# The second block's output projection by seven block products for three of four tile pairs

## The chip, the cores and the metric

The program runs on one core of a Trainium2 chip. The metric is the device time of one execution in microseconds. Five engines work side by side and meet at semaphores: TensorE (matmul), VectorE, ScalarE, GpSimd, and SyncE, which issues most DMAs. In profile rows they are PE (PEld for its weight loads), DVE, ACT, POOL and SP.

## The reference

Two transformer-like blocks follow each other on x of 1024 tokens by 1024 features, in float32. The change is in the second block, at the line that multiplies by w_out:

```
br_a = neighbourhood_attention(q, k, v, rpb) @ w_na_out
br_b = silu(layernorm(conv(c_a * sigmoid(c_b)))) @ w_conv_out
merged = sigmoid(g_a) * br_a + sigmoid(g_b) * br_b
x = x + merged @ w_out
h2 = rmsnorm(x, norm2_g)
up = dwconv3(h2 @ w_up)
gate, val = split(up)
x = x + (gelu(gate) * val) @ w_down
```

merged and w_out are 1024x1024.

## The kernel before

x is kept transposed, as eight tiles x_t[:, d, :] of 128 features by 1024 tokens. Each float32 product is made of three matmuls of a rounded type: high by high, high by low, low by high. So every operand is split first: a rounding makes the high part, a subtraction the low part.

The stages around the change are these.

- The branch stage (TensorE, line 2008). For each of the eight output tiles d TensorE makes both branches, 48 matmuls of 512 columns, into four banks of PSUM. VectorE multiplies each by its gate and adds the two (`merge`, lines 3776 to 3781), ScalarE rounds the merged tile (line 2777) and VectorE makes its low part (`mix2_low`, line 3785).
- The output projection (TensorE, `product`, line 1449). For each of eight tiles of w_out, 8 slices of the contraction x 3 matmuls x 2 halves of the tokens = 48 matmuls. GpSimd splits each weight tile (lines 1261 and 1269), one ahead of TensorE. VectorE adds the result to x (`enter`, line 3345). ScalarE stores x to DRAM, squares it (line 2422), and VectorE sums the squares (`add_alone`, line 3337) for the norm.
- The FFN's first product already uses the seven-product scheme (Winograd's form of Strassen's): a pair of weight tiles and the two halves of the tokens make a 2x2 block product out of seven block products instead of eight. Its operands are direct parts of x (b11, b21, b22) and mixed ones (t1 to t4). VectorE makes their sums and low parts (`h_combos`, lines 3303 to 3325) and ScalarE the high ones (line 2396). The contraction's slices go in pairs of tiles kk and kk+4, in the order 0, 1, 3, 2 (`PAIR_ORDER`), and the tiles of the output projection in the same order (`ORDER`: 0, 4, 1, 5, 3, 7, 2, 6). In `enter` VectorE makes the parts of the first pair after its fourth addition of a tile and those of the second after its fifth; `tile 6` and `tile 7` of the text are the last two in this order.
- Behind them, the loop over FFN pairs: TensorE line 1738, weight sums and low parts on GpSimd (lines 1294 to 1318), high parts on ScalarE (line 2414), convolution taps on VectorE (lines 3836, 3840), GELU on ScalarE (line 2796).

Each engine works through its own list in the order in which the code is written; there is no scheduler.

## Time and profile before

| | us |
|---|---|
| median of 3 runs | 2425.54 |
| lowest, highest | 2425.41, 2428.5 |
| the profiled execution | 2427.07 |
| its span | 2425.3 |
| PE busy | 2401.6 (99%) |
| DVE busy | 1896.2 (78%) |
| ACT busy | 960.4 (40%) |
| POOL busy | 1358.6 (56%) |

The span is what the records cover; the profiled execution's own time is 1.8 us longer. A busy share is an average over stages with different limits, so it doesn't tell what bounds one of them. In every slice of the page but the first TensorE is at 9 tenths.

### The profile page before, as it was taken

To read this page: it belongs to the slowest core of one execution; us is meant where nothing else is said; L and a number is where in the kernel's file an instruction comes from. 1 tells how busy PE (TensorE), PEld (TensorE's weight loads), DVE (VectorE), ACT (ScalarE), POOL (GpSimd) and SP (SyncE) were. 2 spreads that over 40 slices of the span, in tenths; PEclk is the share of its full clock that TensorE was granted. 3 is DMA by queue.
4 is the path that set the end of the run, shared out by engine and by line. 5 is a ranking of instruction groups with operands and counts; after the bars stand their busy time and mean duration, and the time that the engine had idled before them with its cause. 6 is when DMAs were issued, how large, how long until landed. Compare 5 with 4: busy or idle time off the path is not lost.

```text
span 2425.3 us, 37420 instructions
## 1 busy us (share of the span) xinstructions
PE 2401.6 (99%) x13845; PEld 1979.7 (82%) x13845; DVE 1896.2 (78%) x1915; ACT 960.4 (40%) x1319; POOL 1358.6 (56%) x791
## 2 busy tenths in 40 slices
PE   8999999999999999999999999999999999999999
PEld 8788887888888788887877788888888888887887
DVE  6766666776667888888877889354799999999998
ACT  5344445353333533324333331311355455443444
POOL 3322222369887777772322223333379999978786
PEclk9999999999999999999999999999999999999999
DMA  6111112234444755431311111113222222235332
GB/s 228 36 35 43 35 35 97 104 125 157 151 155 172 256 170 155 151 126 36 131 41 35 39 35 52 44 52 124 93 87 78 86 88 85 78 130 183 104 113 92
DMA packets 243636, 244.79 MB, mean 101 GB/s; under 512 B 16943, under 2 KB 212186, under 8 KB 238810
## 3 DMA queue, kind: packets, MB, share of 16 engines
q1 hardware_dynamic: 214916, 166.70, 21.9%
q10 hardware_dynamic: 28630, 76.86, 8.3%
q8 instruction: 59, 0.97, 0.2%
q14 instruction: 31, 0.25, 0.0%
HBM read 181.13 MB, written 64.17 MB: 101 GB/s over the span
## 4 chain that ended last, share of the span: by engine, by line
PE 86%; DVE 8%; ACT 2%; issue 2%; POOL 1%; DMA 0%; DVEq 0%; SPq 0%; ACTq 0%; POOLq 0%
PE psum L1449 30%; PE psum L1738 26%; PE psum L1858 11%; PE psum L2106 7%; PE psum L2008 3%; PE psum L1487 2%; PE psum L1574 1%; PE psum L1512 1%; PE psum L1920 1%; PE psum L1939 1%; DVE x_t L3373 1%; DVE sq_sum_gain L3580 0%; POOL ffn_s_lo L1318 0%; PE psum L1634 0%; DVE sq_sum L3337 0%
## 5 line engine op out<-in xcount | busy, mean ns | idle before, releaser
L1261 POOL CAST w_hi<-w_raw 128x1024 fp32r<-128x1024 f32 x85 | 98.6, 1160 | 769.0 <-issue 386.2
L1449 PE MATMUL psum<-h_hi,w_hi 128*128 128x512 f32 x1040 | 329.9, 398 | 1.3 <-DVE h_lo L3040 1.1
L1449 PE MATMUL psum<-h_lo,w_hi 128*128 128x512 f32 x1040 | 321.5, 390 | 0.0
L1449 PE MATMUL psum<-h_hi,w_lo 128*128 128x512 f32 x1040 | 321.1, 390 | 0.0
L1449 PEld LDWEIGHTS psum<-h_hi,w_lo 128*128 128x128 f32 x1040 | 195.3, 188 | 41.9
L1449 PEld LDWEIGHTS psum<-h_lo,w_hi 128*128 128x128 f32 x1040 | 195.2, 188 | 41.7
L1269 POOL TENSOR_TENSOR w_lo<-w_raw,w_hi 128x1024 fp32r<-128x1024 f32 x85 | 220.0, 2588 | 9.5 <-DVE h_lo L3040 2.8
L1449 PEld LDWEIGHTS psum<-h_hi,w_hi 128*128 128x128 f32 x1040 | 189.2, 188 | 39.5 <-issue 1.8
L3634 DVE SCALAR_TENSOR_TENSOR conv_t<-u_t,cols,conv_t 128x1024 f32<-128x1024 f32 x120 | 175.1, 1459 | 2.6
L1318 POOL TENSOR_TENSOR ffn_s_lo<-ffn_s_sum,ffn_s_hi 128x512 fp32r<-128x512 f32 x84 | 159.8, 1933 | 7.0 <-ACT ffn_s_hi L2414 4.0
L1738 PE MATMUL psum<-ffn_t_hi,ffn_s_hi 128*128 128x512 f32 x252 | 98.0, 389 | 0.0
L1738 PE MATMUL psum<-ffn_t_lo,ffn_s_hi 128*128 128x512 f32 x252 | 98.0, 389 | 0.0
L1738 PE MATMUL psum<-ffn_t_hi,ffn_s_lo 128*128 128x512 f32 x252 | 98.0, 389 | 0.0
L1318 POOL TENSOR_TENSOR mlp_s_lo<-mlp_s_sum,mlp_s_hi 128x512 fp32r<-128x512 f32 x60 | 95.0, 1612 | 2.6 <-ACT mlp_s_hi L2414 2.6
L1858 PE MATMUL psum<-down_part_hi,down_hi_odd 128*128 128x512 f32 x228 | 88.7, 389 | 0.0
L1858 PE MATMUL psum<-down_part_lo,down_hi_odd 128*128 128x512 f32 x228 | 88.7, 389 | 0.0
L1858 PE MATMUL psum<-down_part_hi,down_lo_odd 128*128 128x512 f32 x228 | 88.7, 389 | 0.0
L3490 DVE TENSOR_TENSOR down_part_lo<-down_part_raw,down_part_hi 128x1536 fp32r<-128x1536 f32 (+2 forms) x31 | 70.4, 2270 | 8.5 <-ACT down_part_hi L2550 8.5
L1858 PE MATMUL psum<-down_part_hi,down_hi_even 128*128 128x512 f32 x196 | 76.3, 389 | 0.1
L1858 PE MATMUL psum<-down_part_hi,down_lo_even 128*128 128x512 f32 x196 | 76.3, 389 | 0.0
L1858 PE MATMUL psum<-down_part_lo,down_hi_even 128*128 128x512 f32 x196 | 76.3, 389 | 0.0
L2414 ACT ACTIVATE ffn_s_hi<-ffn_s_sum 128x512 fp32r<-128x512 f32 x84 | 48.3, 624 | 63.8 <-POOL ffn_s_sum L1296 55.8
(625 smaller groups left out, 6865.6 us busy)
## 6 DMA issues: line engine op xcount, KB each, us to landing
w_raw<-in_w_in SPq DMA_DIRECT2D x120, 256.0 KB, 3.0
w_raw<-in_w_up SPq DMA_DIRECT2D x76, 256.0 KB, 3.3
act_parts<-act_mixed ACTq DMA_DIRECT2D x15, 1024.0 KB, 3.8
down_part_raw<-act_parts SPq DMA_DIRECT2D x14, 1024.0 KB, 5.6
down_part_raw<-act_parts SPq DMA_DIRECT2D x15, 768.0 KB, 6.4
ffn_raw<-in_w_up SPq DMA_DIRECT2D x44, 256.0 KB, 3.3
ffn_rows<-ffn_gate ACTq DMA_DIRECT2D x22, 512.0 KB, 2.6
ffn_part_raw<-ffn_rows SPq DMA_DIRECT2D x18, 512.0 KB, 4.3
```

What stands on the lines that cost most here:

```text
L1261: pool.tensor_copy(hi, raw).then_inc(weight_hi, 1)
L1269: pool.tensor_tensor(lo, raw, hi.bitcast(F32), ALU.subtract).then_inc(weight_split, 1)
L1318: done = pool.tensor_tensor(lo[:, :], full[c], hi[:, :].bitcast(F32), ALU.subtract)
L1449: last = pe.matmul(psum[:, first_bank + t, :], w, a[:, k, t * HALF:(t + 1) * HALF], start=(k == order[0] and j == 0), stop=(k == order[-1] ...
L1487: last = pe.transpose(psum[:, dst_bank + c // 4, (c % 4) * P:(c % 4 + 1) * P], block_in, ident[:, :])
L1738: last = pe.matmul(psum[:, bank, :], w, a[:, :], start=start and kk == part[0] and j == 0, stop=stop and kk == part[-1] and j == 2, skip_g ...
L1858: done = pe.matmul(psum[:, bank, :], w, b, start=first and i == 0 and k == 0, stop=last and i == len(window) - 1 and k == 2)
L2008: last = pe.matmul(psum[:, bank + t, :], w, a[:, t * HALF:(t + 1) * HALF], start=(k == 0 and j == 0), stop=(k == 3 and j == 2))
L2106: done = pe.matmul(psum[:, bank, 0:tokens.stop - tokens.start], w, b, start=first and i == 0 and k == 0, stop=last and i == len(window) - ...
L2414: act.activation(stage.weights[s][c][0][:, :], src, ACT.Copy).then_inc(weight_combo_hi, 1)
L3490: dve.tensor_tensor(part_lo[f % 3][:, here, :], part_raw[f % 3][:, here, :], part_hi[f % 3][:, here, :].bitcast(F32), ALU.subtract).then_i ...
L3634: dve.scalar_tensor_tensor(acc, u_t[:, c % 2, tap:tap + SEQ], w, acc, ALU.mult, ALU.add)\
```

## The change

The weight tiles of the output projection are taken in pairs. Three of the four pairs are made by seven block products with the two halves of the tokens, 12 matmuls each (4 pairs of slices x 3), and the fourth (tiles 6 and 7) stays as it was.

- In the branch stage the tiles are merged in the order 0, 4, 1, 5, ... (`MIX_ORDER`), and after each second one VectorE makes four sums, and ScalarE and VectorE the high and low parts of t1 to t4.
- GpSimd makes the factors of a pair (`out_pair_factors`): four sums and seven low parts of 128x512; ScalarE makes the seven high parts (`out_factor_hi`).
- TensorE begins the first pair with what doesn't need the last merged tiles (`ahead2`).
- VectorE adds each block product to every part of x that holds it (`out_pair`): ten additions for a pair.
- The squares of the tiles 1, 2 and 3 go through a buffer of half a tile (`square_halves`).
- The FFN parts of the first two pairs of tiles are made after the third pair of the projection is added, not between the additions.

```diff
+MIX_ORDER = tuple(d for kk in range(KT // 2) for d in (kk, kk + KT // 2))
+MIX_SUMS = ("t1", "t3", "t2", "t4")
+MIX_LOWS = ("t4", "t2", "t1", "t3")
+OUT_PAIRS = 3
+MIX_0, OUT_0, WSUM_0, HIGH_0, FACTOR_0 = 2, 1, 5, 1, 16
+OUT_SEVEN = ("b11", "b21", "t4", "t2", "t1", "b22", "t3")
+OUT_FACTOR = {"b11": "a11", "b21": "a12", "t4": "a22", "t2": "s2", "t1": "s1", "b22": "s4", "t3": "s3"}
+OUT_BANK = {"b11": 0, "t1": 1, "t3": 2, "t2": 3, "t4": 4, "b21": 5, "b22": 6}
+OUT_WSUMS = (("s1", "s2", "s3", "s4"), ("s1", "s2", "s4", "s3"))
+OUT_HIGHS = (("a11", "a12", "s1", "s2", "a22", "s3", "s4"), ("a11", "a12", "a22", "s1", "s2", "s4", "s3"))
+OUT_LOWS = (("a11", "a12", "s1", "s2", "s3", "a22", "s4"), ("a11", "a12", "a22", "s1", "s2", "s4", "s3"))
...
-                ([], KT // 2, lambda i: [branches(i * 2 * P + j * P) for j in range(2)], []),
+                ([], KT // 2, lambda i: [branches(i * P + j * HALF) for j in range(2)], []),
...
+                elif isinstance(n, int) and T_OUT2 + 2 <= n < T_FFN:
+                    sp.wait_ge(weight_split, n - n % 2)
...
+                if i == 0:
+                    add("s1")
+                    low("a11")
+                    low("a12")
+                    pool.wait_ge(tile_done, T_OUT2)
+                    add("s2")
+                    low("s1")
+                    low("s2")
+                    add("s3")
+                    low("s3")
+                    low("a22")
+                    add("s4")
+                    raw_read("a22")
+                    low("s4")
+                    return
+                for name in ("a11", "a12", "a22"):
+                    low(name)
+                out_piece_done(pool, i - 1, "t1")
+                add("s1")
+                add("s2")
+                low("s1")
+                out_piece_done(pool, i - 1, "b22")
+                add("s4")
+                low("s2")
+                out_piece_done(pool, i - 1, "t3")
+                add("s3")
+                raw_read("s2")
+                low("s4")
+                low("s3")
...
-            def out_tile2(d, part=range(KT), split=None):
-                return product(T_OUT2 + d, d % 2, 2 * (d % 2), mix2_hi, mix2_lo, part, split=split)
+            def out_seventh(i, name, part=range(KT // 2)):
+                factor = OUT_FACTOR[name]
+                pe.wait_ge(out_factor, FACTOR_0 + out_nth(OUT_LOWS, i, factor))
+                for kk in part:
+                    if name[0] == "b":
+                        pe.wait_ge(mix_split, KT + 2 * kk + (2 if name[1] == "2" else 1))
+                        p, d, half = mix2_direct(kk, name)
+                        hi, lo = mix2_hi[p, d, half], mix2_lo[p, d, half]
+                    else:
+                        pe.wait_ge(mix_part_lo, MIX_0 + 4 * kk + MIX_LOWS.index(name) + 1)
+                        hi, lo = mix2_parts[kk][name][0][:, :], mix2_parts[kk][name][1][:, :]
+                    at_k = slice(kk * P, (kk + 1) * P)
+                    wh, wl = out_w[factor][0][:, at_k], out_w[factor][1][:, at_k]
+                    for j, (w, a) in enumerate(((wh, hi), (wh, lo), (wl, hi))):
+                        last = pe.matmul(psum[:, OUT_BANK[name], :], w, a, start=kk == 0 and j == 0,
+                                         stop=kk == KT // 2 - 1 and j == 2)
...
+            def out_bank_read(i, name):
+                if name in ("b22", "t3"):
+                    pe.wait_ge(x_added, KT + 2 + 2 * i + (1 if name == "b22" else 2))
+                else:
+                    pe.wait_ge(out_read, OUT_0 + 8 * i + {"b11": 2, "b21": 3, "t4": 4, "t2": 6, "t1": 8}[name])
+            ahead2, last2 = range(KT // 2 - 1), [KT // 2 - 1]
             pe.wait_ge(branch_a, KT - 1)
-            pe.wait_ge(branch_b, KT - 1)
-            out_tile2(0, split=lambda k: (mix_split, KT + k + 1))
-            for d in range(1, KT - 1):
-                if d >= 2:
-                    pe.wait_ge(x_added, KT + 2 + d - 1)
-                out_tile2(d)
-            pe.wait_ge(x_added, KT + 2 + KT - 2)
+            out_seventh(0, "b11", ahead2)
+            pe.wait_ge(branch_a, KT)
+            out_seventh(0, "b21", ahead2)
+            out_seventh(0, "t1", ahead2)
+            pe.wait_ge(branch_b, KT)
+            out_seventh(0, "t2", ahead2)
+            out_seventh(0, "t3", ahead2)
+            out_seventh(0, "b11", last2)
+            out_seventh(0, "b21", last2)
+            out_seventh(0, "t4")
+            out_seventh(0, "t2", last2)
+            out_seventh(0, "t1", last2)
+            out_seventh(0, "b22")
+            out_seventh(0, "t3", last2)
+            for i in range(1, OUT_PAIRS):
+                for name in OUT_SEVEN:
+                    out_bank_read(i - 1, name)
+                    out_seventh(i, name)
+            def out_tile2(d, part=range(KT)):
+                return product(T_OUT2 + d, d % 2, 2 * (d % 2), mix2_hi, mix2_lo, part)
+            out_bank_read(OUT_PAIRS - 1, "t1")
+            out_tile2(KT - 2)
+            out_bank_read(OUT_PAIRS - 1, "t3")
...
+            def square_halves(e):
+                act.wait_ge(x_added, ffn.added + e + 1)
+                spill_x(ORDER[e])
+                if e >= 2:
+                    act.wait_ge(sq_summed, ffn.sums + e - 1)
+                act.activation(sq_half[:, :], x_t[:, ORDER[e], 0:HALF], ACT.Square).then_inc(sq_half_ready, 1)
+                act.wait_ge(sq_half_added, OUT_0 + e)
+                act.activation(sq_half[:, :], x_t[:, ORDER[e], HALF:], ACT.Square).then_inc(sq_ready, 1)
+            square_alone(ffn, 0)
+            square_halves(1)
+            out_arrived(2)
+            out_factor_hi(2, *OUT_HIGHS[1])
+            for e in (2, 3):
+                square_halves(e)
+            out_piece_done(act, OUT_PAIRS - 1, "t3")
+            square_alone(ffn, 4)
+            for kk in PAIR_ORDER[:2]:
+                for names in (DIRECT, MIXED):
+                    h_combos_hi(ffn, kk, names)
+            square_alone(ffn, 5)
+            enter(ffn, 4, 5, eps2, range(KT - 2, KT - 1))
...
+            def mix2_sums(kk):
+                dve.wait_ge(merged, 2 * kk + 2)
+                b11, b12, b21, b22 = (sig_a[:, d, half] for d in (kk, kk + KT // 2) for half in (left_half, right_half))
+                t1, t2, t3, t4 = (mix2_parts[kk][name][2][:, :] for name in ("t1", "t2", "t3", "t4"))
+                dve.tensor_tensor(t1, b12, b11, ALU.subtract).then_inc(mix_summed, 1)
+                dve.tensor_tensor(t3, b22, b12, ALU.subtract).then_inc(mix_summed, 1)
+                dve.wait_ge(mix_summed, MIX_0 + 4 * kk + 2)
+                dve.tensor_tensor(t2, b11, t3, ALU.add).then_inc(mix_summed, 1)
+                dve.wait_ge(mix_summed, MIX_0 + 4 * kk + 3)
+                dve.tensor_tensor(t4, b21, t2, ALU.subtract).then_inc(mix_summed, 1)
...
+            for n in range(KT):
+                merge(n)
+                if n % 2:
+                    mix2_sums(n // 2)
+                    mix2_low(n - 1)
+                    mix2_low(n)
+                    mix2_parts_low(n // 2)
...
+                out_piece_done(dve, i, "b11")
+                add(both[0], twice("b11"))
+                add(both[1], twice("b11"))
+                out_piece_done(dve, i, "b21")
+                add(x_t[:, a, left_half], bank("b21"), after=1)
+                out_piece_done(dve, i, "t4")
+                add(x_t[:, b, left_half], bank("t4"), after=2)
+                for e in ((), (1,), (2, 3))[i]:
+                    square_halves_added(e)
+                out_piece_done(dve, i, "t2")
+                add(x_t[:, a, right_half], bank("t2"), after=1)
+                add(both[1], twice("t2"), after=4)
+                out_piece_done(dve, i, "t1")
+                add(x_t[:, a, right_half], bank("t1"), after=5)
+                add(x_t[:, b, right_half], bank("t1"), after=6)
+                out_piece_done(dve, i, "b22")
+                add(x_t[:, a, right_half], bank("b22"), x_added, after=7)
+                out_piece_done(dve, i, "t3")
+                add(both[1], twice("t3"), x_added, after=8)
 
             dve.wait_ge(x_back, 16 * 2)
-            enter(ffn, lambda e: 2 * (e % 2))
-            left_half, right_half = slice(0, HALF), slice(HALF, SEQ)
+            for i in range(OUT_PAIRS):
+                out_pair(i)
+            for kk, alone in zip(PAIR_ORDER[:2], (4, None)):
+                for names in (DIRECT, MIXED):
+                    h_combos(ffn, kk, names)
+                if alone is not None:
+                    dve.wait_ge(x_added, ffn.added + alone + 1)
+                    add_alone(ffn, alone)
+            enter(ffn, lambda e: 2 * (e % 2), range(KT - 2, KT))
```

VectorE's list at the end of the projection shows the last point. Names: ffn_t_0 and ffn_b_0 are mixed and direct parts of the FFN's first pair, sq a squared tile. Before:

```order
L3345 TENSOR_TENSOR x_t<-x_t,psum 128x1024
L3337 TENSOR_TENSOR sq_sum<-sq_sum,sq 128x1024
L3303 TENSOR_TENSOR ffn_t_0_sum<-x_t 128x512
L3325 SCALAR_TENSOR_TENSOR ffn_b_0_lo<-x_t,cols,ffn_b_0_hi 128x512
L3325 SCALAR_TENSOR_TENSOR ffn_t_0_lo<-ffn_t_0_sum,cols,ffn_t_0_hi 128x512
L3325 SCALAR_TENSOR_TENSOR ffn_b_0_lo<-x_t,cols,ffn_b_0_hi 128x512 x2
L3307 SCALAR_TENSOR_TENSOR ffn_t_0_sum<-x_t,cols,ffn_t_0_scaled 128x512
L3310 SCALAR_TENSOR_TENSOR ffn_t_0_sum<-x_t,cols,ffn_t_0_sum 128x512
L3312 SCALAR_TENSOR_TENSOR ffn_t_0_sum<-x_t,cols,ffn_t_0_sum 128x512
L3323 TENSOR_TENSOR ffn_t_0_lo<-ffn_t_0_sum,ffn_t_0_hi 128x512 x3
L3345 TENSOR_TENSOR x_t<-x_t,psum 128x1024
L3337 TENSOR_TENSOR sq_sum<-sq_sum,sq 128x1024
```

The third pair of VectorE's additions, and what stands behind them now:

```order
L4070 TENSOR_TENSOR x_t<-x_t,psum 128x1024 x3
L4070 TENSOR_TENSOR x_t<-x_t,psum 128x512 x2
L4052 TENSOR_TENSOR sq_sum<-sq_sum,sq_half 128x512
L4054 TENSOR_TENSOR sq_sum<-sq_sum,sq_half 128x512
L4052 TENSOR_TENSOR sq_sum<-sq_sum,sq_half 128x512
L4054 TENSOR_TENSOR sq_sum<-sq_sum,sq_half 128x512
L4070 TENSOR_TENSOR x_t<-x_t,psum 128x512
L4070 TENSOR_TENSOR x_t<-x_t,psum 128x1024
L4070 TENSOR_TENSOR x_t<-x_t,psum 128x512 x3
L4070 TENSOR_TENSOR x_t<-x_t,psum 128x1024
L3531 TENSOR_TENSOR ffn_t_0_sum<-x_t 128x512
L3553 SCALAR_TENSOR_TENSOR ffn_b_0_lo<-x_t,cols,ffn_b_0_hi 128x512
```

(The first of the three additions of 1024 columns belongs to the second pair.) The FFN parts have moved behind six tiles' additions, and two additions a pair have become ten.

On GpSimd, the end of the branch stage's loop and the first weight tile of the projection, before (w_hi and w_lo are the split tile):

```order
L1262 REGISTER_ALU
L1269 TENSOR_TENSOR w_lo<-w_raw,w_hi 128x1024
L870 REGISTER_ALU
L870 COMPARE_AND_BRANCH
L1261 CAST w_hi<-w_raw 128x1024
L1269 TENSOR_TENSOR w_lo<-w_raw,w_hi 128x1024
```

and the factors of the first pair, behind the branch stage's last tile, now (out_w_a are direct factors, out_w_s and out_first_s sums):

```order
L1295 TENSOR_TENSOR out_first_s_700<-w_raw 128x512
L1300 TENSOR_TENSOR out_w_a_lo<-w_raw,out_w_a_hi 128x512 x2
L1295 TENSOR_TENSOR out_first_s_701<-out_first_s_700,w_raw 128x512
L1300 TENSOR_TENSOR out_w_s_lo<-out_first_s_700,out_w_s_hi 128x512
L1300 TENSOR_TENSOR out_w_s_lo<-out_first_s_701,out_w_s_hi 128x512
L1295 TENSOR_TENSOR out_w_s_sum<-w_raw 128x512
L1300 TENSOR_TENSOR out_w_s_lo<-out_w_s_sum,out_w_s_hi 128x512
L1300 TENSOR_TENSOR out_w_a_lo<-w_raw,out_w_a_hi 128x512
L1295 TENSOR_TENSOR out_w_s_sum<-w_raw,out_first_s_701 128x512
L1300 TENSOR_TENSOR out_w_s_lo<-out_w_s_sum,out_w_s_hi 128x512
```

A CAST and a subtraction of a whole tile each have become eleven operations of half a tile for two tiles.

## Rows read from the trace of the kernel before

**Rows 1.** Busy time by stretch: us, then each engine's busy us (x instructions), clock, DMA
```profile
core 0: us, PE busy (x) PEld busy (x) DVE busy (x) ACT busy (x) POOL busy (x), PEclk, DMA share, GB/s
1585.30:1673.00 87.70, 87.13 (x385) 71.81 (x384) 48.40 (x33) 13.54 (x13) 28.65 (x16) 1.00 0.16 48
1673.00:1760.40 87.40, 87.40 (x387) 72.39 (x386) 54.78 (x45) 22.62 (x32) 32.30 (x18) 1.00 0.37 133
```

**Rows 2.** Timeline, PE: start us, us, operation, in brackets the idle time before
```profile
1673.21 0.62 PE L1449 MATMUL psum<-mix_hi,w_hi 128*128 128x512 f32 x2
...
1760.25 0.39 PE L1738 MATMUL psum<-ffn_b_hi,ffn_first_a_hi 128*128 128x512 f32 x1
...
1839.91 0.50 PE L1738 MATMUL psum<-ffn_b_hi,ffn_s_hi 128*128 128x512 f32 x1 [1.56 <-DVE ffn_z_val L3894]
```

**Rows 3.** Waits of PE from 1600 to 2190: us in total, times, longest
```profile
PE psum L1738 <- DVE ffn_z_val L3894: 1.6, 1, 1.6
```

**Rows 4.** Timeline, DVE, around the last addition of a tile
```profile
1758.41 2.30 DVE L3337 TENSOR_TENSOR sq_sum<-sq_sum,sq 128x1024 f32<-128x1024 f32 x1
1760.64 1.21 DVE L3345 TENSOR_TENSOR x_t<-x_t,psum 128x1024 f32<-128x1024 f32 x1
```

**Rows 5.** Chain of waits after it: start us, us, what
```profile
1781.56 1.46 POOL ffn_a_lo L1318
...
1819.64 1.05 ACT ffn_gate L2796
```

**Rows 6.** Timeline, POOL and DVE at the same times
```profile
1767.96 1.29 POOL L1294 TENSOR_TENSOR ffn_s_sum<-ffn_raw 128x512 f32<-128x512 f32 x1 [8.33 <-DMA ffn_raw<-in_w_up]
1769.33 1.60 POOL L1296 TENSOR_TENSOR ffn_s_sum<-ffn_s_sum,ffn_raw 128x512 f32<-128x512 f32 x1
...
1769.84 1.64 DVE L3310 SCALAR_TENSOR_TENSOR ffn_t_sum<-x_t,cols,ffn_t_sum 128x512 f32<-128x512 f32 x1
...
1795.62 2.16 POOL L1296 TENSOR_TENSOR ffn_s_sum<-ffn_s_sum,w_raw 128x512 f32<-128x512 f32 x1
...
1796.54 0.67 DVE L3888 TENSOR_TENSOR third_sum<-second_sum,psum 128x512 f32<-128x512 f32 x1
```

**Rows 7.** Timeline, POOL's split of the last branch tile, and DVE
```profile
1663.78 2.40 POOL L1269 TENSOR_TENSOR w_lo<-w_raw,w_hi 128x1024 fp32r<-128x1024 f32 x1
...
1678.07 2.43 DVE L3785 TENSOR_TENSOR mix_lo<-sig_a,mix_hi 128x1024 fp32r<-128x1024 f32 x2
...
1707.38 3.40 DVE L3337 TENSOR_TENSOR sq_sum<-sq_sum,sq 128x1024 f32<-128x1024 f32 x1
```

**Rows 8.** DMA issues, 1640 to 1800: count, KB each, median us to landing
```profile
w_raw<-in_w_out SPq DMA_DIRECT2D x16, 256.0 KB, 3.0
x_t<-x_spill ACTq DMA_DIRECT2D x1, 4096.0 KB, 13.3
```

**Rows 9.** Timeline, DVE, FFN parts of the first three pairs
```profile
1721.58 0.68 DVE L3303 TENSOR_TENSOR ffn_t_sum<-x_t 128x512 f32<-128x512 f32 x1
1723.40 0.75 DVE L3325 SCALAR_TENSOR_TENSOR ffn_b_lo<-x_t,cols,ffn_b_hi 128x512 fp32r<-128x512 f32 x1 [1.14 <-ACT ffn_b_hi L2396]
...
1728.41 4.82 DVE L3323 TENSOR_TENSOR ffn_t_lo<-ffn_t_sum,ffn_t_hi 128x512 fp32r<-128x512 f32 x3
...
1745.29 1.90 DVE L3323 TENSOR_TENSOR ffn_t_lo<-ffn_t_sum,ffn_t_hi 128x512 fp32r<-128x512 f32 x3
...
1751.97 1.78 DVE L3303 TENSOR_TENSOR ffn_t_sum<-x_t 128x512 f32<-128x512 f32 x1
```

**Rows 10.** Busy time and granted clock (PEclk) around two waits of PE
```profile
384.00:386.00 2.00, 1.00 (x14) 0.88 (x15) 2.00 (x4) 1.81 (x4) 0.90 (x1) 1.00 0.00 0
386.00:388.00 2.00, 2.00 (x8) 1.55 (x7) 1.82 (x3) 1.50 (x3) 1.92 (x2) 0.54 0.03 8
388.00:390.00 2.00, 2.00 (x71) 1.64 (x70) 2.00 (x3) 0.86 (x1) 0.60 (x1) 0.60 0.03 6
...
1840.00:1842.00 2.00, 2.00 (x9) 1.63 (x10) 2.00 (x2) 0.87 (x2) 2.00 (x3) 1.00 0.00 0
```

157 lines of the change are left out of this document (137 added, 20 removed).

## The prediction

> **What bounds the kernel now.** I read the busy shares by stretch first. In the stretch of the output projection TensorE is busy for 87.40 of 87.40 us and VectorE for 54.78 [rows 1], which looks like a stage bound by TensorE. Its first matmul starts at 1673.21 and the first of the next stage at 1760.25 [rows 2]: 87.04 us for 384 matmuls, 0.2267 us each.
>
> The timeline of VectorE says more. It has idle time early in the stage, but none at its end: the addition of squares before the last addition of a tile ends at 1760.71, and that last addition (x_t<-x_t,psum, the eighth) starts at 1760.64 [rows 4] (a record overlaps the next one slightly). TensorE's last tile ended at the same moment. The two engines tie there.
>
> The chain of waits from there on leaves TensorE: last addition, sums for the mixed parts on VectorE, table loads and rounding on ScalarE, low parts on GpSimd, ScalarE's GELU behind them, and VectorE again, until TensorE itself waits 1.56 us at 1839.91 [rows 2, 5]. Between 1600 and 2190 TensorE has no other wait [rows 3]. So the kernel's end moves by as much as this chain moves, and the chain starts with the last addition. I call the start of that addition L; before, L = 1760.64. A TensorE that is done earlier gains nothing unless L is earlier.
>
> **What TensorE saves.** Three pairs by seven block products are 3 x 7 x 4 x 3 = 252 matmuls of 512 columns, and two plain tiles 96: 348 for 384. 36 x 0.2267 = 8.2 us are gone. That is the most that the change can give.
>
> **What a contended operation costs.** The new work is on VectorE and GpSimd, and the rows show that these two hold each other up. A GpSimd half-tile operation (128x512) takes 1.29 us alone, a VectorE one with two SBUF inputs 0.75 [rows 6, 9]; where both have a queue, they alternate, and each takes 1.60 to 1.64 us [rows 6]: with the step between them some 1.7 us for one of each. A VectorE operation of 1024 columns takes 1.2 us alone (2.43 for two), and 3.40 when it meets a whole-tile operation of GpSimd [rows 7]. An addition from PSUM is not held: 0.67 us while GpSimd was in an operation of 2.16 [rows 6].
>
> The Trainium skill (GPSIMD Engine Reference, Key points) says the same of the interfaces: GpSimd contends with VectorE instructions that have two SBUF inputs, and so not with an addition whose second input is PSUM. The trace agrees, with 0.67 us. Were the PSUM additions held too, the sum would be that of the third rival below.
>
> **The branch stage.** Each pair of tiles gets four sums and four low parts of 512 columns more on VectorE, 8 x 0.65 = 5 us, up to 8 when GpSimd splits a weight tile. VectorE was busy for 48.4 of 87.7 us there [rows 1], 39 us idle for four pairs, so three of the four are hidden. ScalarE's four roundings are hidden too (13.5 of 87.7 us). The fourth pair cannot be made before the last branch tile, at 1673.2.
>
> **The first pair, where TensorE waits.** It starts at 1673.2 with 45 matmuls that don't need the fourth pair (10.2 us), but need seven factors from GpSimd. These begin when both weight tiles are there: the split of the last branch tile ends at 1663.78 + 2.40 = 1666.2 [rows 7], the landing takes 3.0 [rows 8] and the two issues 0.9: 1670. Six operations alone (6 x 1.31) bring 1677.9, then two in alternation: the low part of s3 is there at about 1682.7. TensorE wants it after 36 matmuls, at 1681.4: 1.4 us, I take 1.6 with the rounding in between. VectorE: last merge 1673.4 to 1677.6; four sums of which three meet GpSimd, to 1683.4; two whole-tile low parts at 2.1 each, 1685.5 and 1687.7. TensorE wants them at 1684.9 and 1686.2, so it waits 0.7 and 1.5 more. Together 3.8 us. Bounds: 0 (nothing contended, as the two low parts in 2.43 us [rows 7]) and 6 (contended to the last mixed low part).
>
> **The end of the third pair.** 1673.2 + 252 x 0.2267 + 3.8 = 1734.1. VectorE has ten additions for a pair instead of two: four of 1024 and six of 512 columns from PSUM, 4 x 1.17 + 6 x 0.63 = 8.5 us for 2.4. They fit into the 19.0 us that TensorE takes for a pair. In the third pair four half-tile additions of squares stand before the t2 piece, in turns with ScalarE through one buffer: about 7 us with one or two met by GpSimd's split (the sixth tile's). I have VectorE through with them at 1731.0 and with the last addition of the pair at 1735.9, for 1735.6 if it waited for nothing but TensorE. GpSimd needs 11 x 1.31 = 14.4 us for a pair's factors, of 19.0: hidden, since a factor is wanted a pair later. The reload of x_t (13.3 us [rows 8]) starts at 1673.4, for 1678.2 before, and lands at 1687, before VectorE is free at 1691: hidden.
>
> **The tail, which decides.** Before, the FFN parts of the first two pairs of tiles were made between the additions of tiles 4, 5 and 6, so in the time of TensorE's last four tiles. Now they stand behind the whole third pair. From 1735.9 VectorE has: parts of pair 0, 11.6 us before (1721.58 to 1733.2), less 2.9 of contention (4.82 for three low parts that take 1.90 alone) and 0.8 of the wait for ScalarE that was 1.14: 7.9; squares 1.2; parts of pair 1, 11.6 before, to 1745.29 + 1.90 = 1747.2, less 2.8 of contention and all of that wait: 7.7; tile 6 added, 1.2; squares 2.1 (held by GpSimd's first FFN weights); the direct parts of the third pair 4.5 (6.4 before, from 1751.97 to 1758.41; 0.68 + 4 x 0.75 = 3.7 alone); squares 2.2, as the 2.30 before [rows 4, 9]. Sum 26.8, so L = 1762.7. Against 1760.64 that is +2.1 us.
>
> TensorE ends its plain tiles at 1734.1 + 21.8 = 1755.9, and must then wait for VectorE: about 1.3 us for a part of the third pair and 4.2 us for the first low part of the fourth. So the 8.2 us saved are spent as 3.8 us of waits at the head of the stage and 5.5 us at the entry of the next one, 9.3 in all; that TensorE is 1.1 us late there costs nothing by itself, the other 1.0 us of L's shift comes back as a longer wait near 1840.
>
> **Sum.** The profiled execution was 2427.07 us with a span of 2425.30; it would be 2429.2. The median of the runs shown is 1.53 lower, so I forecast 2425.54 + 2.1 = 2427.6. A measurement of this kernel can tell about 0.2% (4.9 us) from no change, and this is less. Range of this case alone: from L with no VectorE operation held at all (first pair's waits 0, so the third pair added by 1731.9, and a tail of 24.1: L = 1756.0, -4.6 us) to L with the larger of all bounds (waits 6, a lag of 2 us more in the third pair: +6 us).
>
> **Rivals.**
>
> 1. TensorE bounds the stage after all, and the saving stays. For it: 99% busy over the span, and no wait in this stage. Against it: L is tied to VectorE, whose tail of 25 us and more would have to fit into the 21.8 us of two tiles. It would give 2425.5 - 8.2 = 2417.4. 6%; another 3% for a part of it beyond 4.9 us.
>
> 2. The clock falls, on the slower side. In a stretch where TensorE waits 2.5 us (one of 1.00 us busy in 2.00 stands in the rows), the granted clock was then 0.54 at 386 to 388 and 0.60 at 388 to 390, mostly the level of 1.2 GHz: 0.46 x 2 + 0.40 x 2 = 1.7 us lost; after the wait of 1.56 us near 1839 it was 1.00 [rows 2, 10]. The waits of the first pair, 1.6, 0.7 and 1.5 us close together, lie between the two. If it falls there, the pairs end 1.7 us later and L moves by about 1.5: +3.6 us, 2429.2. The waits of 1.3 and 4.2 us at the entry of the FFN stage can bring it down too; TensorE would be late by 1.1 + 1.7 = 2.8 us at the place where the chain makes it wait until 1.56 + 2.1 = 3.7 later than before, so that costs nothing. It decides once TensorE is late by more than 3.7 us there: if the low level came twice and lasted twice as long as in the rows, TensorE would be late by 1.1 + 3.4 + 3.4 = 7.9 us, 4.2 beyond that point, so 2427.6 + 4.2 = 2431.8. 25% for the first form, within 0.2% still; 8% for the second.
>
> The Trainium skill (TensorE: Matmul & The Clock Gate, Part 1) says that the array's clock follows how busy it has been, half rate after idleness and full rate when busy. The trace agrees with its 0.54. By that rule alone each of the new waits puts TensorE at risk, which is this rival.
>
> 3. GpSimd holds the PSUM additions as well. Ten additions for a pair at 1.7 for the 0.6 to 1.2 us would make 8.5 into 17 us; with the squares, 5 to 7 us, that is up to 24 us for a pair of TensorE's 19.0, and VectorE begins 7 us after the first piece is done: the third pair would be added some 12 us later, 2440. Against it is the row of 0.67 us. 3%.
>
> **How the numbers follow.** Forecast case: 55%; clock in the first form 25%, in the second 8%; saving kept 9%; PSUM additions held 3%. Faster than 0.2%: the 6 + 3 of the first rival, less 2 for what lies at its edge: 7%. Slower by more than 0.2%: 8 + 3 and 2 from the upper end of the forecast: 13%. Within: 80%. Range 2423.0 to 2431.8: it holds the forecast's own range (2420.9 to 2431.6) but for its lowest 2.1 us, the first form of the clock, and the edge of the second.
>
> **What would show it.** In the profile after: 348 matmuls in the stage; TensorE waiting for GpSimd's low parts and for mix_lo near 1681 to 1688, about 4 us; VectorE nearly without idle time from 1718 to its last addition of a tile, which starts at 1761 to 1765; TensorE's first FFN matmul near 1756 and a wait of 4 us for ffn_b_lo behind it; GpSimd busy for 14 to 16 us in each pair. I am wrong if L lies before 1757, if the waits of the first pair are under 1 or over 6 us, or if TensorE's wait near 1840 doesn't move with L.

## The result and the profile after

The changed kernel takes 2431.06 us, median of 16 runs (2428.5 to 2434.67), and the kernel before 2425.61 (16 runs): a ratio of 1.0022, 95% interval 1.0016 to 1.0029, or 5.4 us (3.9 to 7.0). The forecast was 2427.6, the range 2423.0 to 2431.8. The time lies in the range, near its upper end, and the sign is right. The 2.1 us of the forecast are less than half of what came. Below, a trace means the profile of one execution.

The profiled execution took 2431.7 us with a span of 2429.5, for 2427.07 and 2425.3 before. The work went where the prediction put it. The first row answers to the branch stage, the second to the projection [rows 1]:

```profile
core 0: us, PE busy (x) PEld busy (x) DVE busy (x) ACT busy (x) POOL busy (x), PEclk, DMA share, GB/s
1585.30:1673.00 87.70, 87.13 (x385) 71.84 (x384) 65.32 (x57) 21.28 (x27) 31.58 (x17) 1.00 0.14 43
1673.00:1760.40 87.40, 82.10 (x355) 65.78 (x354) 69.82 (x76) 34.04 (x54) 52.47 (x36) 1.00 0.42 142
```

VectorE has 16.9 us more in the branch stage and TensorE is as busy there as before: that work is hidden. In the projection TensorE is no longer busy all the time. Its waits from 1600 to 2190, where there was the one of 1.6 us [rows 3]:

```profile
engine line waited for: us in total, times, longest us
PE psum L1858 <- DVE ffn_b_lo L3553: 5.1, 2, 3.8
PE psum L2184 <- DVE mix_lo L4017: 1.8, 2, 1.3
PE psum L2184 <- issue: 1.7, 2, 1.2
PE psum L2184 <- POOL out_w_s_lo L1300: 0.9, 1, 0.9
```

The wait near 1840 [rows 2] is not in the list. The timeline of TensorE shows where each of the others stands; the last row is the matmul that waited before:

```profile
1682.23 0.50 PE L2184 MATMUL psum<-mix_t_hi,out_w_s_hi 128*128 128x512 f32 x1 [0.88 <-POOL out_w_s_lo L1300]
1685.12 0.47 PE L2184 MATMUL psum<-mix_hi,out_w_a_hi 128*128 128x512 f32 x1 [0.53 <-DVE mix_lo L4017]
1687.34 0.47 PE L2184 MATMUL psum<-mix_hi,out_w_a_hi 128*128 128x512 f32 x1 [1.29 <-DVE mix_lo L4017]
...
1716.03 0.47 PE L2184 MATMUL psum<-mix_hi,out_w_a_hi 128*128 128x512 f32 x1 [1.20 <-issue]
...
1724.89 0.47 PE L2184 MATMUL psum<-mix_t_hi,out_w_s_hi 128*128 128x512 f32 x1 [0.46 <-issue]
...
1760.83 0.50 PE L1858 MATMUL psum<-ffn_b_hi,ffn_first_a_hi 128*128 128x512 f32 x1 [1.31 <-DVE ffn_b_lo L3553]
...
1767.68 0.79 PE L1858 MATMUL psum<-ffn_b_hi,ffn_first_a_hi 128*128 128x512 f32 x1 [3.83 <-DVE ffn_b_lo L3553]
1768.27 0.63 PE L1858 MATMUL psum<-ffn_b_lo,ffn_first_a_hi 128*128 128x512 f32 x1
1768.70 0.63 PE L1858 MATMUL psum<-ffn_b_hi,ffn_first_a_lo 128*128 128x512 f32 x1
...
1844.52 0.39 PE L1858 MATMUL psum<-ffn_b_hi,ffn_s_hi 128*128 128x512 f32 x1
```

The two rows behind 1767.68 start 0.43 us apart, where a matmul of this size has 0.2267 at full clock: that is the level of 1.2 GHz; the granted clock was 0.50 from 1768 to 1772 (the stretches stand under `warm`). It holds to 1773.8, for 14 matmuls.

On VectorE L, the start of the last addition of a tile, answers to [rows 4]. I had it at 1762.7:

```profile
1733.04 4.73 DVE L4070 TENSOR_TENSOR x_t<-x_t,psum 128x512 f32<-128x512 f32 x6
...
1763.98 1.22 DVE L3573 TENSOR_TENSOR x_t<-x_t,psum 128x1024 f32<-128x1024 f32 x1
```

**A ledger of TensorE.** From here on I measure from S, the stage's first matmul, to L on VectorE, and to M, the matmul that waited near 1840 [rows 2]: S alone moves by 4 us from one execution to the next (1671.35 to 1675.35), so plain times can't be compared. Before, S is 1673.21, L 87.4 us and M 166.7 us later. After, S is 1673.04, L 90.9 and M 171.5 us later: M moved by +4.8.

A wait costs more than its idle time. The matmul before the first wait starts at 1680.97 and the next at 1682.23, 1.26 us later, where matmuls in a row start 0.23 us apart. Of these 1.26 us 0.88 are idle, because the idle time is counted only from the end of the record before, which lasts 0.39 us; and the second matmul behind the wait comes another 0.1 us late. I call this the restart.

With the restarts the ledger reads: saved 8.2; first pair 3.5 lost (2.7 idle); third pair, with the start of the plain tile behind it, 2.5 (1.7 idle); entry of the FFN stage 8.6 (5.1 idle, 2.9 by the clock); the wait near 1840, 1.7 with its restart, gone. That is -8.2 + 3.5 + 2.5 + 8.6 - 1.7 = +4.7, for 4.8.

### The profile page after: what moved, and what is told of

Its sections match the earlier page's. It is cut to its first block, busy times and chain, and to the rows that moved or that the text cites. A ratio compares the mean times of both kernels' runs of the same rounds, so it can differ in the third digit from the quotient of the medians.

```text
span 2429.5 us, 37511 instructions
## 1 busy us (share of the span) xinstructions
PE 2397.2 (99%) x13809; PEld 1973.4 (81%) x13809; DVE 1927.7 (79%) x1974; ACT 982.0 (40%) x1359; POOL 1382.6 (57%) x812
## 4 chain that ended last, share of the span: by engine, by line
PE 87%; DVE 5%; POOL 2%; ACT 2%; DMA 2%; issue 1%; SPq 0%; DVEq 0%; ACTq 0%; POOLq 0%
PE psum L1858 29%; PE psum L1569 28%; PE psum L1978 11%; PE psum L2272 7%; PE psum L2128 3%; PE psum L1607 2%; PE psum L1694 1%; PE psum L1632 1%; PE psum L2040 1%; PE psum L2059 1%; POOL out_w_s_sum L1295 1%; DVE sq_sum_gain L3808 0%; DMA w_raw<-in_w_out 0%; PE psum L1754 0%; DVE sq_sum L3799 0%
## 5 line engine op out<-in xcount | busy, mean ns | idle before, releaser
L1381 POOL CAST w_hi<-w_raw 128x1024 fp32r<-128x1024 f32 x79 | 91.9, 1163 | 712.5 <-issue 341.0
L1389 POOL TENSOR_TENSOR w_lo<-w_raw,w_hi 128x1024 fp32r<-128x1024 f32 x79 | 206.2, 2610 | 9.5 <-DVE h_lo L3268 3.2
L3726 DVE TENSOR_TENSOR down_x<-down_x,psum 128x512 f32<-128x512 f32 x90 | 60.5, 678 | 14.2 <-PE psum L1978 13.9
```

The costliest lines, as they stand in the source:

```text
L1381: pool.tensor_copy(hi, raw).then_inc(weight_hi, 1)
L1389: pool.tensor_tensor(lo, raw, hi.bitcast(F32), ALU.subtract).then_inc(weight_split, 1)
L3726: dve.tensor_tensor(total, total, psum[:, down_bank(p), :], ALU.add).then_inc(product_added, 1)
```

## The experiments

Each run has one trace, from which L - S and M - S are read; the table gives how far they moved from the 87.4 and 166.7 us of the kernel before. Times are compared with runs of the kernel before on the same chip, by the ratio of the runs; the plain difference of the medians is up to 1.1 us away from it (2.8 us for `l_late`, 0.9 for `pairs2`, -0.7 for `pairs2_t4`). An interval is about 2 us to either side, so the traces tell finer than the times.

Two limits of the traces belong here. The kernel before has one trace; `late`, which has the same code up to L, repeats its L - S to 0.01 us. And they are read only up to M: from M to the end of TensorE's last matmul the fourteen traces take 577.7 (`late`) to 579.9 us (before), so a shift of M reaches the end only to within 2.2 us.

| run | L - S | M - S | time against before, us |
|---|---|---|---|
| changed kernel | +3.5 | +4.8 | +5.4 (3.9 to 7.0) |
| again, again_2 | +4.5, +3.2 | +4.0, +3.8 | one execution each |
| late | 0 | +3.7 | +3.6 (1.5 to 5.8) |
| l_late | +2.2 | +2.1 | +1.7 (-0.5 to 4.1) |
| warm | +2.3 | +2.6 | +5.6 (3.4 to 7.8) |
| feed | +2.0 | +1.5 | +4.6 (2.4 to 6.8) |
| fixed3 | +1.9 | +1.1 | +3.2 (1.0 to 5.3) |
| turn | +7.4 | +7.9 | one execution |
| pairs2 | -0.5 | -0.2 | 0.0 (-2.2 to 2.2) |
| pairs2_t4 | -2.1 | -2.9 | -1.5 (-3.6 to 0.7) |
| pairs2_spill | -2.4 | -2.4 | -1.9 (-4.1 to 0.2) |
| best | +0.7 | +0.7 | +1.0 (-1.2 to 3.2) |

### Two chains into the end: late and l_late

Both start from the kernel before. `late` delays TensorE alone, at the entry of the FFN stage; `l_late` delays VectorE alone:

```
                 begin(stage, "a21", "b11", 7)
+                if stage is ffn:
+                    for _ in range(24):
+                        pe.matmul(psum[:, 5, :], stage.first["a11"][0][:, 0:P], stage.h_parts[0]["b11"][0][:, :], ...)
```

> The kernel before, with 24 matmuls of 512 columns more on TensorE at the entry of the FFN stage, between the first products (ahead of the part of the fourth pair of tiles); their sums go to a PSUM bank that nothing reads. 24 x 0.2267 = 5.4 us. Theory A (TensorE and the chain of VectorE, ScalarE and GpSimd that starts at L run side by side, and the later of them ends the kernel): TensorE has 1.56 us of waiting near 1840 to give, so the wait there is gone and the kernel is 5.4 - 1.6 = 3.9 us longer. Theory B (the chain alone sets the end, as long as L stays): L stays at 1760.6 and the time is within 0.5 us of before. Theory C (every matmul counts, nothing is hidden): +5.4 us.

```
+                    if stage is ffn and e >= KT - 2:
+                        dve.tensor_tensor(banks(4), x_t[:, ORDER[e - 1], :], x_t[:, ORDER[e - 1], :], ALU.add)
                     dve.wait_ge(tile_done, stage.tile - KT + e + 1)
```

> The kernel before, with two VectorE additions of 1024 columns more (1.22 us each; two SBUF inputs, into a PSUM bank that nothing reads), one ahead of the addition of the seventh tile and one ahead of that of the eighth. Nothing else is changed. Theory A (the chain from L sets the end, and TensorE waits for it near 1840): L is 2.4 us later, TensorE's wait near 1840 grows from 1.6 to 4.0 us, and the kernel is 2.4 us longer, more if the clock falls in that longer wait. Theory B (TensorE sets the end): the time stays within 0.5 us, since TensorE's own first products of the FFN stage don't need the last tile until later. At the entry TensorE may wait a few tenths for the fourth pair's low part.

In `late` L did not move, M moved by 3.7 of the 5.4 us added, and TensorE waits nowhere between 1600 and 2190. M is this row, with S at 1671.92:

```profile
1842.36 0.39 PE L1738 MATMUL psum<-ffn_b_hi,ffn_s_hi 128*128 128x512 f32 x1
```

That is theory A's 3.9, and theory B (only L counts) falls. In `l_late` M moved by 2.1 with L's 2.2, and that is theory A too; the time alone (-0.5 to 4.1) doesn't tell it from theory B. Two details were not as expected: TensorE waited 1.1 us for the fourth pair's low part already at the entry, so its wait at M was 2.0 and not 4.0, and right behind that the clock fell:

```profile
1842.93 0.69 PE L1738 MATMUL psum<-ffn_b_hi,ffn_s_hi 128*128 128x512 f32 x1 [1.96 <-DVE ffn_z_val L3896]
```

```profile
1840.00:1844.00 4.00, 2.04 (x8) 0.89 0.00 0
1844.00:1848.00 4.00, 4.00 (x14) 0.69 0.32 131
```

So M is set by the later of two: TensorE, with 1.6 us to give in the kernel before, and the chain from L, which takes 78.4 to 79.6 us in the traces where TensorE waits at M. In `again`, `again_2`, `feed`, `turn` and `pairs2_t4` TensorE waits for the same chain one FFN pair earlier, near 1825, for 0.3 to 0.5 us, and M comes 78.5 to 79.8 us behind L.

### The clock at the entry: warm

The changed kernel, with 17 such matmuls in the wait of 3.83 us.

> The changed kernel, with 17 matmuls of 512 columns (3.9 us) put where TensorE waits 3.83 us for the first low part of the fourth pair at the entry of the FFN stage; their sums go to a PSUM bank that nothing reads. Theory A (the clock fell because TensorE stood still there, and its 3.4 to 3.7 us made TensorE later than the chain's slack): the granted clock stays at 1.00 from 1764 to 1776, the next product starts at about 1767.7 as without them, L stays at 1764.0, TensorE is 3.5 us earlier by 1780 and again waits near 1843, for about 2.3 us, since the chain now is the later one (L + 3.3 against before); the kernel is 1.3 us shorter than the changed one, some 4 us longer than before. Theory B (the chain from L alone explains the loss): no change against the changed kernel. Theory C (the clock falls here whatever TensorE does): the granted clock is 0.5 to 0.8 again and nothing is gained.

```profile
1764.00:1768.00 4.00, 0.32 (x1) 0.87 0.02 2
1768.00:1772.00 4.00, 4.00 (x10) 0.50 0.96 307
1772.00:1776.00 4.00, 4.00 (x15) 0.77 0.28 85
```

These are the changed kernel's stretches (us, busy, granted clock, DMA share, GB/s), and these are warm's:

```profile
1764.00:1768.00 4.00, 3.97 (x18) 1.00 0.24 69
1768.00:1772.00 4.00, 4.00 (x20) 1.00 1.03 322
1772.00:1776.00 4.00, 4.00 (x15) 1.00 0.02 7
```

TensorE at M in warm:

```profile
1842.20 0.50 PE L1858 MATMUL psum<-ffn_b_hi,ffn_s_hi 128*128 128x512 f32 x1 [1.63 <-DVE ffn_z_val L4202]
```

The low level is gone and the wait at M is back. TensorE's standing still brought the clock down; theories B and C fall. The fall cost TensorE 2.8 us at the entry, but M gained 2.2, and 1.2 of that came by an L that was earlier in this execution. What the clock costs at M is so an estimate of about 1 us: with the changed kernel's L and warm's chain of 79.5 us M would lie 170.5 us behind S, for 171.5. The time does not show even that: 2430.78 for 2431.06. The profiled execution was the fourth fastest of eleven (2428.93); what the slower ones lost isn't seen in it. That `warm`, `feed` and `fixed3` are 2 to 3 us slower by time than their traces say at M stays open.

### What delays the third pair: feed, again, again_2

The two waits of 1.20 and 0.46 us have no engine as their releaser. The loads stand behind them. SyncE, ScalarE and GpSimd of the changed kernel:

```profile
1704.28 4.06 SPq L1054 DMA_DIRECT2D w_raw<-in_w_out  x4
...
1713.56 1.67 ACT L2952 ACTIVATE out_w_a_hi<-w_raw 128x512 fp32r<-128x512 f32 x3 [5.34 <-DMA w_raw<-in_w_out]
1714.66 3.76 POOL L1300 TENSOR_TENSOR out_w_a_lo<-w_raw,out_w_a_hi 128x512 fp32r<-128x512 f32 x3 [7.66 <-ACT out_w_a_hi L2952]
...
1724.74 1.30 POOL L1295 TENSOR_TENSOR out_w_s_sum<-w_raw 128x512 f32<-128x512 f32 x1
1726.11 0.94 SPq L1054 DMA_DIRECT2D w_raw<-in_w_out  x2
```

A pair's raw tiles come free only when GpSimd has read them last (its last sum), the next four loads start then, and only then does GpSimd have work again. From 1704.28 to 1726.11 this loop takes 21.8 us, for TensorE's 19.0 for a pair. The edit frees them earlier for the third pair and moves two spills of x behind the loads:

```
 (GpSimd, second pair)        low("s1"), add("s4"), low("s2"), add("s3"), raw_read
                          ->  add("s4"), add("s3"), raw_read, low("s1"), low("s2")
 (ScalarE)                    spill_x(ORDER[0]), spill_x(ORDER[1])  behind  out_arrived(2)
```

> The changed kernel with the raw weight tiles of the third pair fetched earlier: GpSimd makes the second pair's sums before its low parts of s1 and s2, so that the raw tiles come free two operations earlier (about 2.5 us), and the spills of the first two x tiles are issued behind the landing of the third pair's weights instead of beside them. Theory A (the loop of load and GpSimd work, 21.8 us a pair, delays the third pair): TensorE's waits at 1716.0 and 1724.9 (1.66 us) go, the half squares stand ahead of TensorE's pieces, the third pair is added at about 1735.7 for 1737.7, L is at 1762.0 for 1764.0, and the kernel is 1.8 to 2.0 us shorter than the changed one. Theory B (VectorE's and ScalarE's turns with the half squares delay the third pair): the two waits go but the third pair is added no more than 0.5 us earlier, and L and the time stay within 0.5 us.

```profile
PE psum L1863 <- DVE ffn_b_lo L3562: 4.5, 2, 4.0
PE psum L2189 <- DVE mix_lo L4026: 1.8, 2, 1.3
PE psum L2189 <- POOL out_w_s_lo L1300: 0.9, 1, 0.9
PE psum L2189 <- issue: 0.6, 1, 0.6
```

The third pair's waits are gone. The 0.6 that is left stands at 1705, in the second pair: the new order makes the low part of s2 late there. The third pair is added 1.8 us earlier behind S and L comes 1.5 us earlier, for the 2.0 of theory A and the 0.5 of theory B. The time doesn't show it (+4.6 for +5.4, each to 2 us).

> The changed kernel itself, one more profiled execution, to see which of its waits repeat. Theory A: the waits of the first pair (0.9, 0.5, 1.3 us) and of the entry (1.3, 3.8) are the same within 0.2 us, since engines alone set them; the two of the third pair (1.2 and 0.5 us) hang on a transfer and vary by a microsecond, and L with them; whether the clock falls at the first pair, at the entry or at both varies. Theory B: all of them repeat within 0.2 us.

> The changed kernel itself, a third profiled execution. In the first two, L was 90.9 and 91.9 us behind the start of the stage (87.4 before) and TensorE's matmul near 1840 at 171.5 and 170.7 (166.7 before). Theory A (what repeats is the mechanism: the waits of the first pair, those of the third pair and those of the entry, and a clock at its low level once in the stage): L at 90.5 to 92.5, that matmul at 170 to 172, first pair's waits 2.7 us, the low level either at the first pair or at the entry. Theory B (the two were chance): outside of these.

The first pair's waits (0.9, 0.5, 1.3) and the entry's (1.3, 3.8 to 4.0) repeat. The third pair's were 1.20 and 0.46, 1.00 and 0.47, 0.86 and 0.43 in the three traces, and 0 and 0.44 in warm, which has the same code up to there: they hang on transfers. In warm the last of the third pair's four loads landed 39.1 us behind S, for 40.5 in the changed kernel, and L came 1.2 us earlier with no edit ahead of it. The low level stood at the entry in all three, at a cost of 1.4 to 2.9 us.

So four traces of the same code have L at +2.3, +3.2, +3.5 and +4.5, and feed's +2.0 lies only 0.3 us outside of them. That the load delays the third pair rests on the waits that go when it lands earlier, in `feed` by the edit and in `warm` by itself; how much `feed` gives, one trace doesn't tell.

A second thing moves L. The last sum of squares ahead of it starts 0.3 us behind the start of a GpSimd operation each time, and takes 1.22 us in three of the four traces and 2.31 in `again`, in `feed` and in `fixed3`:

```profile
1762.84 1.22 DVE L3565 TENSOR_TENSOR sq_sum<-sq_sum,sq 128x1024 f32<-128x1024 f32 x1
```

```profile
1763.65 2.31 DVE L3565 TENSOR_TENSOR sq_sum<-sq_sum,sq 128x1024 f32<-128x1024 f32 x1
```

The first row is the changed kernel's, the second again's. L moves by 1.1 us with it.

### Two engines side by side: turn

```
                     low("s1")
+                    pool.wait_ge(mix_split, 2 * KT)
                     low("s2")
```

> The changed kernel, where GpSimd, after the low part of s1 in the first pair, waits until VectorE has made its four sums and the two whole-tile low parts (mix_lo), so that the two engines work one after the other there. Theory A (the long VectorE operations of this place, 1.64 to 1.77 us a sum and 2.2 a low part, are long because GpSimd is at work beside them): the sums take 0.7 us each and the two low parts 2.43 together, mix_lo is done at about 9.5 us behind the start of the stage for 14.1, and GpSimd's operations take 1.3 us; TensorE waits 4 us for the low part of s2 and 2.6 more for that of s3 and none for mix_lo, so that the first pair is 3 to 4 us longer: in turns the engines are quicker one by one and later in all. Theory B (the operations are long by their own form): VectorE's durations stay.

VectorE in the changed kernel (S = 1673.04):

```profile
1676.95 1.68 DVE L4025 TENSOR_TENSOR mix_t_sum<-sig_a 128x512 f32<-128x512 f32 x1
1678.55 1.77 DVE L4026 TENSOR_TENSOR mix_t_sum<-sig_a 128x512 f32<-128x512 f32 x1
1680.36 0.69 DVE L4028 TENSOR_TENSOR mix_t_sum<-sig_a,mix_t_sum 128x512 f32<-128x512 f32 x1
1681.09 1.64 DVE L4030 TENSOR_TENSOR mix_t_sum<-sig_a,mix_t_sum 128x512 f32<-128x512 f32 x1
1682.76 4.43 DVE L4017 TENSOR_TENSOR mix_lo<-sig_a,mix_hi 128x1024 fp32r<-128x1024 f32 x2
```

and with GpSimd silent (S = 1673.01):

```profile
1676.93 0.69 DVE L4026 TENSOR_TENSOR mix_t_sum<-sig_a 128x512 f32<-128x512 f32 x1
1677.54 0.69 DVE L4027 TENSOR_TENSOR mix_t_sum<-sig_a 128x512 f32<-128x512 f32 x1
1678.26 0.69 DVE L4029 TENSOR_TENSOR mix_t_sum<-sig_a,mix_t_sum 128x512 f32<-128x512 f32 x1
1678.98 0.69 DVE L4031 TENSOR_TENSOR mix_t_sum<-sig_a,mix_t_sum 128x512 f32<-128x512 f32 x1
1679.71 2.36 DVE L4018 TENSOR_TENSOR mix_lo<-sig_a,mix_hi 128x1024 fp32r<-128x1024 f32 x2
```

Theory A holds to a tenth: 0.69 for three sums of 1.64 to 1.77, and 2.36 for 4.43. In turns VectorE is done 5.1 us earlier, but GpSimd's work comes later by as much, TensorE waits 4.2 us for the low part of s2 and its clock falls behind that, 7.2 us lost in the first pair for 3.5. M is 3.1 us later than in the changed kernel. Side by side, each slowed, is the better choice here. The wait for s2 in `turn`:

```profile
1683.51 0.77 PE L2185 MATMUL psum<-mix_t_hi,out_w_s_hi 128*128 128x512 f32 x1 [4.22 <-issue]
```

### The tail: pairs2, pairs2_t4, fixed3

`pairs2` sets OUT_PAIRS to 2: two pairs by seven products and four plain tiles. The FFN parts and squares of the first tiles stand between the additions of the plain ones again. `pairs2_t4` begins t4 (nine matmuls that don't need the fourth pair of tiles) ahead of the last quarter of b11. `fixed3` is three pairs with warm's, feed's and t4's edits.

> The changed kernel with two tile pairs by seven block products and four plain tiles (360 matmuls, 24 fewer than before). The FFN parts of the first two pairs of tiles then stand beside the plain tiles again. Theory A (the loss is the tail behind the third pair and what it does to TensorE): TensorE waits 2.7 us at the first pair and nowhere else in the stage, and nothing at the entry of the FFN stage, the clock stays at 1.00, L is at 1758.3 (1760.6 - 5.4 + 2.7 + some 0.5 of restarts), and the kernel is 2 to 2.5 us shorter than before, 7 to 8 shorter than the changed one. Theory B (the loss is the extra work of VectorE and GpSimd wherever it stands, in part in the branch stage and the first pair): L is at 1760.6 or later and the time is that of before or up to 3 us more.

> Two pairs by seven products and four plain tiles, and in the first pair the first nine matmuls of the t4 piece stand ahead of the first use of the fourth pair of tiles. In the run with two pairs TensorE lost 1.0 us at the low part of s3, 0.7 and 1.5 us at mix_lo and 1.5 us at the low level of the clock right behind, and VectorE then stood idle for 2.56 us ahead of the last addition. Theory A (TensorE bounds this version at L): the two waits for mix_lo shrink from 2.2 to about 0.5 us, the clock is less likely to fall there, L is 1.7 us after less the same (85.2 us behind the start of the stage for 86.9), up to 3.2 earlier if the clock stays up, and the kernel is 1.7 to 3 us shorter than with two pairs alone. Theory B (VectorE or the chain behind L bounds it): L moves by no more than 0.5 us and the time with it.

> Three pairs as in the changed kernel, with all three of its repairs: raw tiles of the third pair fetched earlier, the t4 piece begun ahead, and 17 matmuls in the wait at the entry of the FFN stage. Theory A (the tail of 26 us behind the third pair bounds what is left): TensorE's waits in the stage are under 1.5 us before the plain tiles, the third pair is added 3 us earlier than in the changed kernel, L is 87.4 to 88.2 us behind the start of the stage (87.4 before, 90.9 changed), the clock stays up, and the kernel is within 1 us of before: repaired, three pairs give nothing, since the tail must still be gone through. Theory B (the saved matmuls come through once the waits are gone): 3 us or more shorter than before.

In `pairs2` there is no wait at the entry, the clock is 1.00 there, and VectorE waits for TensorE ahead of its last addition:

```profile
1760.04 1.22 DVE L3572 TENSOR_TENSOR x_t<-x_t,psum 128x1024 f32<-128x1024 f32 x1 [2.56 <-PE psum L1569]
```

That is theory A's place. L came 0.5 us earlier and not 2.3, since TensorE lost 5.1 us in the first pair and not 3.2; the time, 0.0 us (-2.2 to 2.2), is that of theory B. The clock fell there this time:

```profile
1688.00:1692.00 4.00, 4.00 (x12) 0.58 0.76 220
```

With t4 ahead that pair cost 2.5 us and the clock stayed up; L and M are 2.1 and 2.9 us earlier than before. `fixed3` put L 1.9 us after that of before (expected 0 to 0.8; the second pair has a new wait of 1.4 us for a bank that VectorE reads late, and the last sum of squares took 2.31 us for 1.22) and won nothing: theory B, the saving coming through, falls. TensorE began the FFN stage 83.1 us behind S there, 4.0 earlier than before, and L still came at 89.3. With fewer savings and no tail behind them, pairs2_t4 is 3.9 us better at M than three pairs with every repair that I had. Dropping the third pair takes its load and its half squares away as well as the tail; no run parts them.

### Two attempts beyond: best, pairs2_spill

> Two pairs by seven products and four plain tiles, with the first pair put in another order: GpSimd makes the low part of a22 ahead of the sum and the low part of s3, TensorE begins t4 ahead of t3 and b22 ahead of the last quarter of b21, the raw tiles of the first plain tile come free two GpSimd operations earlier, and the first two spills of x stand behind their landing. In the run before this (two pairs, t4 begun ahead) TensorE lost 1.15 us at the low part of s3, 1.1 at the fourth pair of tiles and 0.7 at the first plain tile's weights. Theory A (TensorE bounds this version up to L): these 3.0 us fall to 1.0 to 1.3, L is at 83.5 us behind the start of the stage for 85.3 (87.4 before), TensorE's matmul that follows the chain near 1840 is at 162.0 to 163.0 for 163.8 (166.7 before), and the kernel is 3.5 to 4.5 us shorter than before. Theory B (the extra work of VectorE bounds it): L does not move by more than 0.5 us.

> Two pairs by seven products and four plain tiles, the t4 piece begun ahead, and the spills of the first two x tiles issued behind the landing of the first plain tile's weights instead of beside it. In the run without that last edit ScalarE issued the two spills at 1703.7, together with the four loads that came next, and TensorE lost 0.7 us at the first plain tile's weights. Theory A (TensorE bounds this version up to L, and the loads land earlier without the spills): that wait is gone, L is at 84.6 us behind the start of the stage for 85.3, the matmul near 1840 at 163.1 to 163.8, and the kernel is 2 to 3 us shorter than before. Theory B (the transfers don't hinder each other): the wait stays at 0.6 us, L at 85.3, and the kernel is 1 to 2.5 us shorter than before.

`best` did not bring what it was built for. In the first pair its waits only changed place (0.56 for s3, 1.41 for s4), and feed's order, which served the third pair, delays s2 in the second by 1.87 us, after which the clock fell (eight matmuls 0.43 us apart). `pairs2_spill` did its part: the wait for the first plain tile's weights (0.6 us in pairs2_t4) is gone, a wait of 0.5 us at the second pair's s2 came with it. M - S is 164.3, for an expected 163.1 to 163.8, since TensorE now reaches M early and waits 1.3 us for the chain. At 2423.37 us and a ratio of 0.9992 (0.9983 to 1.0001) it has the lowest time here. It is probably but not certainly faster than before, and can't be told from pairs2_t4 (0.9994, 0.9985 to 1.0003).

## Why the prediction was right and where it was off

**What bounds it** held, with an addition. M moves with L (`l_late`) as long as TensorE has time to give, and by TensorE beyond that (`late`, whose time, +3.6 us, 1.5 to 5.8, bears it out at the end). In the changed kernel the two arrive nearly together: M - L is 80.5, 78.8 and 79.8 us in its three traces, for a chain of 78.4 to 79.8. In the first TensorE is the later, in the other two it has waited for the chain near 1825.

**The branch stage** hidden, as said: TensorE 87.13 of 87.70 us.

**The first pair** was put at 3.8 us of waits, 1.6 for s3 and 0.7 and 1.5 for mix_lo. Measured: 0.88, 0.53, 1.29 idle, 2.7 us, or 3.5 with the restarts, which I had not counted as such. The contention that I took for it is shown by `turn`. The two low parts took 4.43 for my 4.2.

**The third pair** is the term that was mis-sized most: I had TensorE waiting for nothing there, because GpSimd's 14.4 us fit into 19.0. The work does take about that (eleven operations of 1.29), but the step left out that its input is a buffer that it must itself set free. Load, wait and work come one after another, 21.8 us a pair. ScalarE's half squares stood behind the late factors as well, and so the pair was added at 1737.7 and not 1735.9. That is 1.8 us of L. `feed` gave 1.5 back, in one trace and with the scatter said above.

**The tail** was 26.8 us and measured 26.3. VectorE is idle for 0.4 us of it, in `fixed3` for 0.7: nothing else sets its length. It is what spends the saving: with three pairs repaired L is still late (`fixed3`), and with two pairs it is not.

**The entry** had its waits right, 1.3 and 4.2 for 1.31 and 3.83. The clause on the clock there (1.7 us lost, and "that costs nothing") was off in size: 2.9 us in the first trace, 1.4 in the other two. With the third pair's 2.5 it made TensorE as late as the chain or later, so the wait near 1840, which I had at 2.6 us, was gone. `warm` gives about 1 us as its price at M.

**Sum.** L by 3.5 (3.2 and 4.5 in the other traces, 2.3 in `warm`) for 2.1, and up to 1.3 more by TensorE. The forecast's 2.1 lies outside the interval of 3.9 to 7.0. The measured 5.4 lies beyond the bound of 0.2% (4.9 us), on which I had put 13%, though the interval holds both sides. That the time is still in the range is partly luck: its upper end was worked out from a clock that falls twice, and what came near it was one fall and the third pair's delay, for which the sum had 0.3 us.

**The signs.** There are 348 matmuls, L is at 1763.98 and the first pair's waits are 2.7 us, as said. TensorE's first FFN matmul is at 1758.0 for 1756, by the third pair's delay. VectorE "nearly without idle time from 1718" did not come: it stands idle for 7.6 us between 1718 and 1733, and is full only behind the third pair. The last sign of being wrong, that the wait near 1840 doesn't move with L, came by its letter: the wait did not grow, it vanished. `l_late`, where it grew from 1.56 to 1.96 us beside 1.1 us of waiting at the entry, and M moved with L, shows the link that it was meant to test.

**Rivals.** TensorE-bound with all saved: no, it waits 9.5 us. PSUM additions held by GpSimd: no; in the third pair six of them took 4.73 us. The clock, as its first form, at the first pair: not in the three traces of the changed kernel, but in `pairs2` and `turn`, 1.5 us and more each. As its second form, TensorE later than the chain: in one of the three traces, by up to 1.3 us, with one fall where I had wanted two. At the entry the clock fell in every trace with a wait of 3.8 us or more.

## What to carry to other kernels

A saving on the engine that is busy all the time counts only if what its results set off can keep pace; list what stood beside the work that goes, and see where it stands now. For a producer that fits into its consumer's time, check its own input buffer too: one set means load and work in series, and the loop is their sum. Put fewer savings where other work covers their tail rather than more savings where none does, and judge an order by each place where it applies, since the one that helped the third pair hurt the second.

## What I had not expected of the hardware

- After a wait the loss is larger than the idle time: with 0.88, 1.29 and 1.20 idle TensorE lost 1.15, 1.53 and 1.44 us, the second matmul behind the wait included.
- The granted clock fell after waits of 0.9, 0.5 and 1.3 us within 6 us in one trace (`pairs2`) and not in five others of the same pattern. After single waits of 1.47 to 1.67 us at M it stayed up in four traces; after 1.87 (`best`), 1.96 (`l_late`) and each of 3.8 us or more it fell. 6 to 14 matmuls then started 0.43 us apart, 1.4 to 2.9 us lost each time.
- In the first pair contention cost VectorE no more than about GpSimd's work beside it: four sums and two low parts took VectorE 10.2 us for 5.1 alone, while GpSimd made four operations of 1.29 alone, 5.2 us, and parts of two more.
- The same two operations beside each other, started 0.3 us apart, took VectorE 1.22 us and GpSimd 2.62 in `again_2`, and VectorE 2.31 in `again`: which engine is held changes from one execution of the same code to the next.
